# Token blocks of x by vector transposes and DRAM transfers, and three late bc convolutions, in a hybrid SSD, S5 and ConvFFN block

## What is computed

```python
xbc = jax.nn.silu(causal_dwconv(xbc, conv_w, conv_b))       # 4 taps
xs, bm, cm = jnp.split(xbc, [D_INNER_A, D_INNER_A + gn], axis=-1)
dt = jax.nn.softplus(dt_raw + dt_bias); a = -jnp.exp(a_log)
X = xh * dt                                   # x per head, tokens x 64
decay_in = jnp.exp(segsum(a * dt))            # 256 x 256 per head
cb = jnp.einsum("bclgn,bcsgn->bgcls", Cc, Bc) # per group
y_diag = jnp.einsum("bgcls,bgrcls,bcsgrp->bclgrp", cb, decay_in, X)
y = (y_diag + d_skip * xh) * silu(z)          # then a norm over each group
```

## Time and profile before

| | |
|---|---|
| median of 3 runs | 1679.96 us (1679.75 to 1681.75) |
| the profiled execution | 1680.3 us, its span 1678.6 us |
| granted TensorE clock, mean | 0.998 of full speed |
| PE / DVE / ACT / POOL busy | 99% / 79% / 57% / 13% of the span |
| zx begins to gate turn 0 | about 60 to 431 us |
| gate turns | about 431 to 642 us |
| DVE busy from 398 to 441 us | 42.8 of 43.0 us |
| DVE / ACT busy from 441 to 635 us | 178.3 / 127.3 of 194 us |

### The profile page before, as it was taken

How to read it: one execution, slowest core, us unless ns; L and a number is a source line. 1 busy time by engine, 2 the same in 40 slices (tenths; PEclk the granted TensorE clock), 3 DMA queues, 4 the chain that set the end, 5 groups by cost and what they waited for, 6 DMA issues and landing times.

```text
span 1678.6 us, 24422 instructions
## 1 busy us (share of the span) xinstructions
PE 1667.1 (99%) x8340; PEld 1395.1 (83%) x8340; DVE 1320.3 (79%) x1685; ACT 962.7 (57%) x1271; POOL 216.4 (13%) x310
## 2 busy tenths in 40 slices
PE   9999999999999999999999999999999999999997
PEld 8888888888788888888888888888888888888886
DVE  7999999999998986545775868888878888845555
ACT  7676676766666667444557755444444444454553
POOL 7843342221000000000000200000000000000001
PEclk9999999999999999999999999999999999999999
DMA  7666766666666566656786577777777777666653
GB/s 254 213 197 199 204 206 200 193 188 190 194 217 231 191 219 189 199 191 201 239 254 232 174 233 241 243 241 244 242 244 241 245 232 248 225 194 195 191 189 123
DMA packets 174569, 358.49 MB, mean 214 GB/s; under 512 B 16880, under 2 KB 39584, under 8 KB 174368
## 3 DMA queue, kind: packets, MB, share of 16 engines
q1 hardware_dynamic: 162528, 338.26, 62.5%
q0 software_dynamic: 11248, 18.37, 4.6%
q10 hardware_dynamic: 720, 0.93, 0.2%
HBM read 335.41 MB, written 15.80 MB: 209 GB/s over the span
## 4 chain that ended last, share of the span: by engine, by line
PE 73%; DVE 2%; issue 0%; ACT 0%; DVEq 0%
PE psum L1822 22%; PE psum L1823 22%; PE psum L1824 22%; PE psum L1783 3%; PE psum L1785 2%; PE psum L1908 1%; DVE wlo L1107 0%; PE psum L1909 0%; DVE vn L1749 0%; PE psum L1933 0%; DVE bc L1303 0%; PE psum L1829 0%; PE psum L1924 0%; DVE dec L1416 0%; PE psum L1982 0%; PE psum L1979 0%
## 5 line engine op out<-in xcount | busy, mean ns | idle before, releaser
L1107 DVE TENSOR_TENSOR wlo<-raw,whi 128x1024 fp32r<-128x1024 f32 x580 | 709.6, 1230 | 321.3 <-ACT whi L666 314.0
L666 ACT ACTIVATE whi<-raw 128x1024 fp32r<-128x1024 f32 x580 | 611.9, 1058 | 577.1 <-PE psum L1824 455.1
L1783 PE MATMUL psum<-act,whi 128*128 128x512 f32 x1088 | 342.5, 396 | 0.0
L1822 PE MATMUL psum<-whi,nw 128*128 128x512 f32 x704 | 274.1, 389 | 0.0
L1824 PE MATMUL psum<-whi,nw 128*128 128x512 f32 x704 | 273.9, 389 | 0.0
L1823 PE MATMUL psum<-wlo,nw 128*128 128x512 f32 x704 | 273.9, 389 | 0.0
L1785 PEld LDWEIGHTS psum<-act,wlo 128*128 128x128 f32 x1088 | 204.4, 188 | 48.3
L1785 PE MATMUL psum<-act,wlo 128*128 128x256 f32 x1088 | 213.7, 278 | 0.0
L1783 PEld LDWEIGHTS psum<-act,whi 128*128 128x128 f32 x1088 | 165.6, 189 | 3.3 <-issue 2.8
L1824 PEld LDWEIGHTS psum<-whi,nw 128*128 128x128 f32 x704 | 132.1, 188 | 27.6
L1822 PEld LDWEIGHTS psum<-whi,nw 128*128 128x128 f32 x704 | 132.1, 188 | 27.3
(11 more groups left out here) (251 smaller groups left out, 2300.3 us busy)
## 6 DMA issues: line engine op xcount, KB each, us to landing
raw<-in_w_up SPq DMA_DIRECT2D x176, 512.0 KB, 4.9
raw<-in_w_zx SPq DMA_DIRECT2D x96, 512.0 KB, 3.7
raw<-in_w_down SPq DMA_DIRECT2D x88, 512.0 KB, 3.8
raw<-in_w_gate SPq DMA_DIRECT2D x64, 512.0 KB, 5.6
raw<-in_w_proj SPq DMA_DIRECT2D x48, 512.0 KB, 4.4
raw<-in_w_bc SPq DMA_DIRECT2D x32, 512.0 KB, 3.7
raw<-in_w_glu SPq DMA_DIRECT2D x32, 512.0 KB, 4.4
raw<-in_w_out SPq DMA_DIRECT2D x32, 512.0 KB, 4.8
```

What stands on the lines that cost most here:

```text
L666: fn(whi[:, s, :], raw[:, s, :], ACTF.Copy).then_inc(hi_ready, 1)
L1107: V.tensor_tensor(wlo[:, s, :], raw[:, s, :], whi[:, s, :], ALU.subtract).then_inc(lo_ready, 1)
L1783: mm(psum[:, b + t, :], whi[:, s, cols(t)], x, start=first, stop=False)
L1822: mm(banks[:, t, :], x_hi, high[:, k], start=j == 0 and k == 0, stop=False)
```

## The change

x no longer goes through PE. DVE transposes 32 x 32 blocks of the group's x into `xblk` (`x_turned`, two instructions of 128 x 384). Four DMAs write the blocks to DRAM, one reads them back as 128 tokens by 768 (`xraw`). ACT scales them by dt into `xtok`, twelve ACTIVATEs of 64 columns (`tokens`). For groups 0 and 1 the transposes stand ahead of bc, the DMAs in SP's queue; for the others the transposes stand in the turn before, the DMAs in POOL's queue around the decay loads. B is used where it lies, so `bst` and `xst` are gone. The space of the blocks is that of bc's later groups: the convolutions of groups 5 and 6 are done in gate turns 1 and 2 (`late_tap`, `late_conv`, `late_silu`), out of `bc` into other places, and that of group 7 moves behind `lo(4)` of turn 0. `bc_count` gives the new count at which a group's convolution is done. bc's loop on SP is written out.

```diff
+        late_bc = {5: bc5, 6: cpad}
+        late_count = {7: 6, 5: 7, 6: 8}
+        def bc_of(g, t):
+            return late_bc[g][:, t, 0:L] if g in late_bc else bc[:, g, t, :]
+        def bc_count(g):
+            return 12 + late_count.get(g, g + 1)
+        def comes_late(name, i, r):
+            return name == "bc" and i == 1 and r in (1, 2)
...
+            def first_tokens_write(g):
+                sp.wait_ge(x_blocks, g + 1)
+                for a in range(4):
+                    sp.dma_start(tokens_at[g, :, :, a, :].rearrange("q j x -> j q x"),
+                                 xblk[g][32 * a:32 * a + 32, :, :, :, :].rearrange("j q k t i -> j q (k t i)")
+                                 ).then_inc(first_written, 16)
+            def first_tokens_fetch(g):
+                sp.wait_ge(first_written, 128)
+                if g == 0:
+                    sp.wait_ge(cz_ready, 16)
+                else:
+                    sp.wait_ge(y5_ready, 8)
+                sp.dma_start(xraw[g][:, :, :, :, :].rearrange("p a k t i -> p (a k t i)"),
+                             tokens_at[g].rearrange("q j a x -> (q j) (a x)")).then_inc(first_read, 16)
...
+                        if j == 6:
+                            first_tokens_write(0)
+                        if j == 7:
+                            first_tokens_write(1)
+                        if j == 24:
+                            first_tokens_fetch(0)
...
+                        if name == "gate" and j == 8:
+                            first_tokens_fetch(1)
...
-            with pool.Fori(0, GROUPS - 1) as i:
-                for half in range(2):
-                    pool.wait_ge(y_ready, i * 2 + (half + 1))
-                    load_decay(i + 1, half)
+            def token_write(g):
+                pool.wait_ge(x_blocks, g + 1)
+                for a in range(4):
+                    pool.dma_start(tokens_at[g % 2, :, :, a, :].rearrange("q j x -> j q x"),
+                                   xblk[g][32 * a:32 * a + 32, :, :, :, :].rearrange("j q k t i -> j q (k t i)")
+                                   ).then_inc(x_written, 16)
+            def token_fetch(g):
+                pool.wait_ge(x_written, 64 * (g - 1))
+                if g > 1:
+                    pool.wait_ge(xtok_ready, g)
+                pool.dma_start(xraw[g][:, :, :, :, :].rearrange("p a k t i -> p (a k t i)"),
+                               tokens_at[g % 2].rearrange("q j a x -> (q j) (a x)")).then_inc(x_read, 16)
+            for i in range(GROUPS - 1):
+                if i:
+                    token_write(i + 1)
+                pool.wait_ge(y_ready, i * 2 + 1)
+                load_decay(i + 1, 0)
+                if i:
+                    token_fetch(i + 1)
+                pool.wait_ge(y_ready, i * 2 + 2)
+                load_decay(i + 1, 1)
...
+            def late_tap(g):
+                act.wait_ge(sum_ready, phase("bc")[4] + g + 1)
+                for t in range(2):
+                    ins = fn(bc_of(g, t), bc[:, g, t, :], ACTF.Identity,
+                             scale=col("conv_a_w", (24 + 2 * g + t) * 4 + 3), bias=col("conv_a_b", 24 + 2 * g + t))
+                ins.then_inc(tap_ready, 1)
+            def late_silu(g):
+                act.wait_ge(conv_done, bc_count(g))
+                to = late_bc[g][:, :, 0:L]
+                fn(to, to, ACTF.Silu).then_inc(xbc_done, 1)
...
-                def stage(g):
-                    fn(bst[:, :], bc[:, ds(g, 1), 0, :].rearrange("p o n -> p (o n)"), ACTF.Copy).then_inc(staged, 1)
-                    fn(xst[:, :, :], zx[:, ds(g * TPG, TPG), 1, :], ACTF.Copy).then_inc(staged, 1)
+                def tokens(g, k):
+                    act.wait_ge(x_read if g > 1 else first_read, 16 * (g - 1) if g > 1 else 16 * g + 16)
+                    for hd in range(HPG):
+                        a = hd % 2 * 2
+                        ins = fn(xtok[:, k, 64 * hd:64 * hd + 64].rearrange("p (a i) -> p a i", a=2),
+                                 xraw[g][:, a:a + 2, k, hd // 2, :], ACTF.Identity,
+                                 scale=dtt[:, k, g * HPG + hd:g * HPG + hd + 1])
+                    if k == 1:
+                        ins.then_inc(xtok_ready, 1)
 
                 if prev is None:
 
                     hi(0)
                     act.wait_ge(x5_ready, 32)
                     act.wait_ge(y5_ready, 8)
-                    act.wait_ge(xbc_done, 16)
-                    stage(0)
                     group_tap("bc", 1, 3)
                     hi(1)
                     hi(2)
-                    group_silu("bc", 1, 3)
-                    act.wait_ge(xbc_done, 20)
-                    act.wait_ge(z_done, 12)
                     decay(0)
                     hi(3)
                     decay(1)
+                    act.wait_ge(dtt_ready, 1)
+                    tokens(0, 0)
+                    tokens(0, 1)
                 else:
                     hi(0)
                     decay(0)
                     hi(1)
+                    tokens(i, 0)
+                    tokens(i, 1)
                     decay(1)
                     group_root(prev)
                     hi(2)
...
                 if prev is not None:
                     group_hi(prev)
                 hi(4)
+                if prev is None:
+                    group_silu("bc", 1, 3)
+                    act.wait_ge(xbc_done, 18)
+                    act.wait_ge(z_done, 12)
+                if i in (1, 2):
+                    late_tap(i + 4)
                 hi(5)
-                if not last:
-                    act.wait_ge(cb_ready, i + 1)
-                    act.wait_ge(xp_ready, i + 1)
-                    stage(i + 1)
                 hi(6)
+                if i in (1, 2):
+                    late_silu(i + 4)
...
+            def late_conv(g):
+                dve.wait_ge(tap_ready, bc_count(g))
+                for k in (2, 1, 0):
+                    for t in range(2):
+                        if k < 2:
+                            step.hold(but=1)
+                        to = bc_of(g, t)[:, 3 - k:L]
+                        ins = V.scalar_tensor_tensor(to, bc[:, g, t, 0:L - 3 + k],
+                                                     col("conv_a_w", (24 + 2 * g + t) * 4 + k), to, ALU.mult, ALU.add)
+                        if k or not t:
+                            step.begun(ins)
+                ins.then_inc(conv_done, 1)
...
+            def x_turned(g):
+                if g < 2:
+                    dve.wait_ge(xbc_done, 2 + g)
+                elif g == 2:
+                    dve.wait_ge(y5_ready, 8)
+                elif g == GROUPS - 1:
+                    dve.wait_ge(xbc_done, 12)
+                if g > 2:
+                    dve.wait_ge(x_written, 64 * (g - 2))
+                for k in range(2):
+                    ins = V.transpose(xblk[g][:, :, k, :, :].rearrange("p q t i -> p t q i"),
+                                      zx[:, TPG * g:TPG * g + TPG, 1, k * P:k * P + P]
+                                      .rearrange("p t (q i) -> p t q i", q=4))
+                ins.then_inc(x_blocks, 1)
+            x_turned(0)
+            x_turned(1)
...
-                def tokens():
+                def mask_cb():
                     dve.wait_ge(cb_ready, i + 1)
-                    V.tensor_tensor(cbm[:, :], CB, mask_in[:, :], ALU.mult)
-                    dve.wait_ge(xp_ready, i + 1)
                     if prev is None:
-                        step.done(V.tensor_copy(dtt[:, :, :], DTT))
-                    for k in range(2):
-                        ins = V.tensor_tensor(
-                            xtok[:, k, :].rearrange("p (h n) -> p h n", h=HPG),
-                            XP[k].rearrange("p (h n) -> p h n", h=HPG),
-                            dtt[:, k, ds(i * HPG, HPG)].rearrange("p (h o) -> p h o", o=1).to_broadcast([P, HPG, 64]),
-                            ALU.mult)
-                    step.done(ins)
+                        V.tensor_copy(dtt[:, :, :], DTT).then_inc(dtt_ready, 1)
+                    step.done(V.tensor_tensor(cbm[:, :], CB, mask_in[:, :], ALU.mult))
 
                 if prev is None:
                     lo(0)
                     group_sums("bc", 1, 3)
                     s5_out(7, YS5_LAST)
                     scan(0)
-                    group_conv("bc", 1, 3)
                     lo(1)
                     lo(2)
                     scan(1)
                     lo(3)
-                    tokens()
+                    mask_cb()
                     blocks(0)
                     blocks(1)
                 else:
...
                     scan(1)
                     if first_scan:
                         lo(1)
-                    tokens()
+                    mask_cb()
                     blocks(0)
                     blocks(1)
                     if not first_scan:
                         lo(1)
+                    if i < GROUPS - 1:
+                        x_turned(i + 1)
```

(20 more changed lines are left out.)

42 lines of the change are left out of this document (32 added, 10 removed).

## The result

The changed kernel takes **1684.66 us** (median of 20 runs, 1683.46 to 1686.81), the kernel before 1680.13 in the same sessions (20 runs): a ratio of 1.0026, 95% interval 1.0020 to 1.0032. It is 4.5 us slower; the forecast was 1684.7.

A forecast was written before the change was run, and what follows sets the result against it. PE, busy 99% of the span, was taken as the bound, with ACT's chain in turns 0 to 3 making it wait: 10.4 us of waits against 5.7 saved, 4.7 slower, forecast 1684.7 us, range 1674.5 to 1692.

The forecast's parts named there:

- Savings, 5.7 foreseen: On PE: 4.6 us of transposes, the 0.76 us wait at unit 5 and the 0.4 us state-sum wait would go.
- The 0.4 us for the state sum: PE's wait for the S5 state sum would go because DVE enters gate turn 0 4.9 us lighter.
- bc edit 0, upper end 0.3: Ahead of bc: DVE's four added block transposes cost PE 0 us, at most 0.3, judged by unit 26's 1.1 us margin.
- Price of a token ACTIVATE: On ACT: one small ACTIVATE about 0.33 us, twelve a turn 3.0 us, with ends 2.4 and 4.7.
- Turn 0: PE waits 1.1 us for unit 9's low half and 1.3 us for the sum of squares.
- Turn 1: PE waits 3.1 us at unit 14 behind tokens and second exp, and 1.7 us at the squares behind group 5's convolution.
- Turns 2 and 3: PE waits 0.7 us before unit 22, 1.8 at the squares behind group 6's convolution, 0.7 before unit 30.
- such turns are PE's: From turn 4 on, the 11.9 us chain from first scan to lo(2) fits; those turns keep the 0.6 us saved.
- rival (c): The transport through POOL's queue bounds every turn; five turns each lose 1.2 us or more, 1690.7 us; chance 0.18.
- Rival (b): Half and half: stalls come to 3 to 9 us, within 3.4 us of before, around 1681; chance 0.22.
- (a): Relief wins: PE's margins in turns 0 and 1 hold, 5.7 us saved, 1674.3 us; chance 0.18.
- (d): The change doesn't do what it says: the transposes' replacement could only fail to hide; nothing left as chance.

The follow-up runs named there:

- experiment 5: The kernel before with its 48 PE transposes of x left out and nothing put in their place: 1676.81 us against 1680.45, 3.6 us faster.
- experiment 2: The changed kernel with five of the twelve token ACTIVATEs left out in each of turns 1 to 7: 1681.36 us, 0.5 above the kernel before.
- experiment 4: The changed kernel with tokens multiplied on POOL (six instructions a turn) instead of ACT: 1682.32 us, 1.4 above the kernel before.
- experiment 12: The changed kernel with convolutions of groups 5 to 7 put back, tokens of turns 1 to 7 on POOL, sum of squares in its own bank: 1676.71 us against 1680.35.
- experiment 9: The changed kernel with convolutions and Silus of groups 5, 6 and 7 back where they stood before: 1680.79 us, 0.3 above the kernel before.
- experiment 3: The changed kernel with five of six DVE instructions of each late convolution (groups 5 and 6) left out: 1683.08 us, 2.2 above the kernel before.
- experiment 11: The changed kernel with POOL tokens, own bank, group 7's convolution back, and half a late convolution in each of turns 2 to 5: 1684.78 us.
- experiment 10: The changed kernel with convolutions of groups 5 to 7 put back, all tokens on POOL, sum of squares in its own bank: 1679.42 us against 1680.53.

## Why the prediction was right, and where not

The time and the side were right; several steps were not, and their errors cancelled. That the time was met so closely is luck.

**Savings, 5.7 foreseen.** The transposes were worth 5.0 us on PE (0.62 a turn at the ends of the units, where I had 0.58), but 3.6 in the time and 3.0 in the trace of experiment 5; I had every microsecond saved come out, as if no other engine were close. The 0.76 us at unit 5 did go. The 0.4 us for the state sum was put in the wrong place: it was in bc, DVE's transposes made it 0.95, and the step "bc edit 0, upper end 0.3", checked at unit 26 alone, missed it by 0.5 us, and "bc shows no PE wait" was wrong. The place to look was the wait that the page already listed.

**Price of a token ACTIVATE, 0.33 us and 3.0 for twelve.** Right (the trace has 333 ns and 2.96 us), as were DVE's transposes of 384 columns with 0.53 to 0.63:

```profile
L948 ACT ACTIVATE xtok<-xraw,dtt x96: 330/333/348, 451.2 to 634.3; 128x64 f32<-128x64 f32 x96
```

**Turn 0.** Unit 9: 1.1 foreseen, 0.6 measured (the weight load's 0.63). The step up to lo(5) was right (462.0 foreseen, 461.8 measured), but PE came 0.4 later, since bc had cost its 0.5. Squares: 1.3 and 1.07.

**Turn 1.** 3.1 at unit 14: it came as 1.07 in front of the heads and 1.71 at the unit, 2.78. The sum is right and the chain (tokens, second exp, two table loads, hi(2)) is the one named; experiments 2 and 4 confirm it. The squares: 1.7 and 1.50.

**Turns 2 and 3.** Here the steps failed: 0.7, 1.8 and 0.7 foreseen at unit 22, the squares of group 2 and unit 30; measured 0, 0.56 and 0. In their place heads waited 1.27 and 1.25 for the Ln. I followed the chain behind the second exp only to hi(2), and not to the Ln that stands between, on which PE waits earlier.

**From turn 4 on "such turns are PE's".** Wrong for turns 5 and 6 (1.08 and 0.63 for the Ln). Turns 5, 6 and 7 took 26.4, 26.0 and 25.6 us (end of a turn's last unit on PE to the next one's), above the 25.5 that I had named as the sign of rival (c). But its cause is not there: DVE waited for decay loads 0.3 us in all eight turns together, and POOL's writes, waits and loads fitted:

```profile
480.18 2.21 POOL L676 DMA_DIRECT2D token_blocks<-xblk  x4 [19.98 <-DVE xblk L1521]
482.39 0.56 POOL L491 DMA_DIRECT2D dec<-decay_rows  x1
484.46 0.55 POOL L685 DMA_DIRECT2D xraw<-token_blocks  x1 [1.52 <-DMA token_blocks<-xblk]
485.00 0.54 POOL L491 DMA_DIRECT2D dec<-decay_rows  x1
```

Four writes cost POOL 2.2 us; the prediction had 2.8 with the gaps. Rival (b) fell only just: it ends at 3.4 us from the kernel before, and the measured 4.5 has 3.4 to 5.4 as its interval. (a) and (d) fell too: (a)'s point, the chain from dt's copy to lo(5) under 9.5 us, was not reached: it took 10.9 (450.94 to 461.80).

**The table load.** The trace of the changed kernel has the reload ahead of turn 2's first exp (497.62, 1.28 us) and the exp 0.02 us behind it. DVE's scan for it had ended at 498.42, so that 0.5 us of the reload were not hidden, and they stand in the chain that ends in the heads' wait of 1.27. The Trainium skill (ScalarE: Activation LUTs, What ACT_TABLE_LOAD costs) has 2.66 us with a drain; by this row, as by the earlier trace rows, the 1.28 stands:

```profile
497.62 1.28 ACT L941 ACT_TABLE_LOAD   x1
498.92 1.17 ACT L941 ACTIVATE dec<-dec 128x1152 f32<-128x1152 f32 x1
```

**The whole, by the runs.** The kernel of experiment 12 is 3.6 us faster than the kernel before: the relief, less what DVE's transposes in bc and POOL's work cost. The tokens on ACT, with the Ln in the shared bank behind them, cost 3.9 (experiment 9 against 12). The moved convolutions cost 4.2 (the changed kernel against experiment 9), 1.7 of them by group 7's place and 2.5 by groups 5 and 6. These are steps from one kernel to the next, so that they add up to the 4.5 measured by themselves; each is uncertain by some 2 us. The prediction has the same two costs and the same relief, with 10.4 us of waits against 5.7 saved, where the runs have 8.1 against 3.6: both sides were about 2 us too high. The tokens' place and the bank change together between experiments 9 and 12 and were not separated there. Nor was what of the 2.5 us is due to DVE's extra 2.44 us a turn and what to the table loads for Silu; experiment 3, with DVE's part gone and ACT's left, points to DVE (2.3 us in the medians, 1.4 between the two traces).

## What to carry to other kernels

Where one engine is busy 99% and the next is busy 24 of 26 us in each turn, a microsecond taken from the first is worth a microsecond only until the second's next deadline, and work moved onto the second is not free because it is idle for 2 us of 26: 4.0 us of convolution on DVE were worth 2.3 (experiment 3), and the halves of experiment 11 cost more than they last. An engine that is busy only 58% can be as dear, where its work stands ahead of something that PE waits for (experiment 2). First look for an engine that is idle in that stretch (POOL here), and ask when its result is wanted (turn 0 of experiment 10). When work is put into a chain, follow every release inside the chain and not only its end; a shared PSUM bank, nearly harmless while a reader is early, becomes a wait. A wait that the page lists must be found on the timeline before it is booked as saved, and the weight loads' waits must be read beside the matmuls'. A long wait of PE can cost more than its length: behind 2.72 and 3.05 us of idle time the granted clock was at its lower level for some 3.4 us, behind 1.71 us (the changed kernel) and 2.23 us (experiment 3) it was not.
